# Down products of a macaron decoder layer: two of three hidden groups through seven half products, added straight from PSUM

## What is computed

```python
x = layer_norm(ALPHA * x + 0.5 * swiglu(x, ffn1_wg, ffn1_wu, ffn1_wd), ln1_g, ln1_b)
z = x @ w_in                                  # 5632 channels: C, B, h, p, g_a, g_p
m = sigmoid(g_a) * (B * conv3(C * h)) + sigmoid(g_p) * y_p     # y_p: pooling branch
x = layer_norm(ALPHA * x + m @ w_out, ln2_g, ln2_b)
x = layer_norm(ALPHA * x + 0.5 * swiglu(x, ffn2_wg, ffn2_wu, ffn2_wd), ln3_g, ln3_b)
# swiglu(x, wg, wu, wd) = (silu(x @ wg) * (x @ wu)) @ wd
```

## Time and profile before

| | |
|---|---|
| Median of three runs | 1075.14 us (1073.98 to 1077.36) |
| Profiled execution | 1076.68 us, span 1074.9 us |
| Mean granted TensorE clock | 0.992 |
| TensorE busy | 1057.1 us, 98%, 8740 matmuls |
| VectorE busy | 634.7 us, 59% |
| ScalarE busy | 436.1 us, 41% |
| GpSimd busy | 528.4 us, 49% |

### The profile page before, as it was taken

The page is one execution under the profiler, slowest core; times in us unless marked ns, Lnnn a source line. Parts: engine busy times, 40 slices in busy tenths (PEclk is TensorE's granted clock), DMA queues, the critical chain, the costliest instruction groups (busy, mean ns, idle before and its releaser), DMA issues.

```text
span 1074.9 us, 20737 instructions
## 1 busy us (share of the span) xinstructions
PE 1057.1 (98%) x8740; PEld 1051.6 (98%) x8740; DVE 634.7 (59%) x910; ACT 436.1 (41%) x659; POOL 528.4 (49%) x310
## 2 busy tenths in 40 slices
PE   7999999999999999999999999999999999999998
PEld 7999999999999999999999999999999999999997
DVE  6988711278845866722524226889884115886386
ACT  3554532155543342332332324445455123455234
POOL 4365554245657344844553546325565432565340
PEclk9999999999999999999999999989999999999999
DMA  8133244233355040532332334103335323333312
GB/s 251 37 110 102 77 118 118 79 99 111 92 142 147 2 123 2 161 99 84 97 100 84 99 111 129 41 1 99 106 93 137 88 70 99 111 91 105 99 51 80
DMA packets 195057, 103.29 MB, mean 96 GB/s; under 512 B 4420, under 2 KB 193492, under 8 KB 194957
## 3 DMA queue, kind: packets, MB, share of 16 engines
q1 hardware_dynamic: 194883, 101.85, 33.4%
q10 hardware_dynamic: 82, 0.12, 0.1%
HBM read 99.74 MB, written 2.48 MB: 95 GB/s over the span
## 4 chain that ended last, share of the span: by engine, by line
PE 89%; DVE 7%; issue 1%; ACT 1%; DMA 1%; POOL 0%; DVEq 0%; POOLq 0%; ACTq 0%
PE ps L1375 14%; PE ps L1372 14%; PE ps L1373 14%; PE ps L1355 14%; PE ps L1357 14%; PE ps L1356 14%; DVE x L1191 1%; DVE xl L956 1%; PE ps L1497 1%; DVE x L1176 1%; DMA raw<-in_ffn_wd_dram 1%; PE ps L1418 1%; PE ps L1425 1%; DVE form_lo L1007 1%; PE ps L1419 1%
## 5 line engine op out<-in xcount | busy, mean ns | idle before, releaser
L571 POOL TENSOR_TENSOR wl<-raw,wh 128x512 fp32r<-128x512 f32 x120 | 227.7, 1925 | 217.4 <-DVE raw L982 171.5
L619 ACT ACTIVATE wh<-raw 128x1024 fp32r<-128x1024 f32 (+3 forms) x203 | 238.4, 1178 | 192.7 <-DMA raw<-in_ffn_wd_dram 103.6
L1355 PE MATMUL ps<-form_hi,wh 128*128 128x260 f32 x640 | 181.5, 284 | 3.2 <-ACT temps L619 3.2
L1357 PE MATMUL ps<-form_hi,wl 128*128 128x260 f32 x640 | 181.1, 283 | 0.0
L1356 PE MATMUL ps<-form_lo,wh 128*128 128x260 f32 x640 | 180.9, 283 | 0.0
L1372 PE MATMUL ps<-xh,wh 128*128 128x260 f32 x640 | 167.0, 282 | 0.7 <-ACT yp L619 0.7
L1373 PE MATMUL ps<-xl,wh 128*128 128x260 f32 x640 | 166.5, 282 | 0.0
L563 POOL TENSOR_TENSOR wl<-raw,wh 128x1536 fp32r<-128x1536 f32 (+2 forms) x36 | 108.4, 3023 | 104.0 <-ACT wh L619 103.9
L1372 PE MATMUL ps<-hid_hi,wh 128*128 128x260 f32 x544 | 141.9, 282 | 0.0
L1373 PE MATMUL ps<-hid_lo,wh 128*128 128x260 f32 x544 | 141.8, 283 | 0.0
L1355 PE MATMUL ps<-xh,wh 128*128 128x260 f32 x480 | 136.1, 284 | 1.2 <-POOL wl L571 1.2
(11 more groups left out here) (240 smaller groups left out, 2304.1 us busy)
## 6 DMA issues: line engine op xcount, KB each, us to landing
raw<-in_ffn_wg_dram SPq DMA_DIRECT2D x80, 256.0 KB, 3.2
raw<-in_w_in_dram SPq DMA_DIRECT2D x40, 512.0 KB, 3.9
raw<-in_ffn_wd_dram SPq DMA_DIRECT2D x16, 768.0 KB, 5.3
b<-in_ffn_wu_dram SPq DMA_DIRECT2D x40, 256.0 KB, 3.4
raw<-in_ffn_wu_dram SPq DMA_DIRECT2D x40, 256.0 KB, 3.0
raw<-in_ffn_wd_dram SPq DMA_DIRECT2D x16, 640.0 KB, 5.4
raw<-in_w_out_dram SPq DMA_DIRECT2D x7, 512.0 KB, 4.0
xrow<-in_x_prompt_dram SPq DMA_DIRECT2D x4, 512.0 KB, 6.6
```

Of the source, the lines that this page charges most:

```text
L571: nc.gpsimd.tensor_tensor(wl_slot[:, s, :], raw_slot[:, s, :], wh_slot[:, s, :].bitcast(F32), ALU.subtract).then_inc(lo_ready, 1)
L619: return nc.scalar.activation(out, in_, ACT.Copy)
L1355: mm(out, hi, vh, start=start and n == 1, stop=False, skip_group_check=more)
L1357: ins = mm(out, lo, vh, start=False, stop=n == count, skip_group_check=more)
```

## The change

The 22 hidden blocks are cut in three groups of 8, 6 and 8 (`GROUPS`). The down products of the first two groups are no longer plain: two output tiles (`j`) against the group's even and odd hidden blocks form a 2 x 2 block matrix, and seven half products replace eight, exactly as for the up products. Each such "down unit" uses the machinery of an up unit: `UNITS` is the list of 28 units of an FFN, 20 up and 8 down, the four down units of a group standing behind the first up unit of the next group. `kblocks` is 4 for up units and for those of the first group, 3 for the second.

The tokens' side of the 2 x 2 matrix wants four combinations of hidden blocks. VectorE makes them from PSUM as the blocks come (`mid_sums`: one operation of 260 columns for an even block, three for an odd one), ScalarE rounds them (`round_mid`), VectorE subtracts (`mid_rest`: 3 x 260 columns, and 260 of the fourth). Of an even block only the first token half is kept as it is. The partial results of a down unit aren't copied out: VectorE adds or subtracts each of the seven straight from PSUM to or from x (`down_add`, 260 columns each), and TensorE then goes on accumulating in the same bank, after a wait for that addition. The third group (8 blocks instead of 10) stays plain, with two weight slots a tile and its lo parts in two pieces.

Other edits: T1 and T3 go to PSUM banks 6 and 7 from the third unit on; T2 is read from there, and ScalarE rounds them only after T2 is made. On VectorE the weight sums are spread out: T1/T3, T2, `rest_thirteen`, T4, then `hid_pair`, and `rest_twenty_four` moves behind `up_first`. On ScalarE the rounding of T1/T3 and of B11, B21, B22 moves ahead. At the end, the twelve extra transposes (`KEEP_WARM`) go, the square root is taken before the copy of the mean, the scale by gamma moves from VectorE to ScalarE, so that VectorE has four operations of 520 columns instead of eight of 260, and the sums of the last tile go between the transposes.

```diff
+    GROUPS = (8, 6, 8)
+    UNITS = [None]
+    for g in range(len(GROUPS)):
+        for f in range(max(GROUP_AT[g], 2), GROUP_AT[g] + GROUPS[g]):
+            UNITS.append(("up", f))
+            if g and f == GROUP_AT[g]:
+                UNITS += [("down", g - 1, j) for j in range(K // 2)]
...
+        def thirteen_whole(n, p):
+            return ps[:, 6:8, 0:kblocks(p) * P] if p > 2 else thirteen(raw_slot, n, p)
...
+            def round_thirteen(n, p):
+                act.wait_ge(t2_made if p > 2 else t13_made, unit_no(n, p))
+                if p > 2 and free[n, "T1", p]:
+                    act.wait_ge(w_used, max(free[n, "T1", p], free[n, "T3", p]))
+                copy(thirteen(wh_slot, n, p), thirteen_whole(n, p)).then_inc(t13_round, 1)
...
+                    keep(first_p, x_bank, "P1", p_taken)
+                    round_thirteen(n, p + 1)
+                    keep(first_q, z_bank, "Q5", q_taken)
+                    round_unit(n, p + 1)
+                    if was[0] == "up":
+                        second_gate(p - 1)
+                    keep(first_u, x_bank, "P6", u_taken)
+                    if was[0] == "up":
+                        hid_up(was[1], p % 2)
...
+                def mid_sums(f, pair):
+                    ...
+                    first = step.on(stt(mid32[:, 1, i, :], fourth_whole(i), -1.0, bank(pair, 1), ALU.mult, ALU.subtract))
+                    tt(mid32[:, 0, i, :], even32[:, 1, :], bank(pair, 1), ALU.subtract)
+                    dve.wait_ge(s.mid_step, first)
+                    tt(mid32[:, 2, i, :], mid32[:, 1, i, :], bank(pair, 0), ALU.add).then_inc(s.mid_made, 1)
...
+                def unit_steps(p):
+                    if was[0] == "up":
+                        up_second(p - 1)
+                    weight_sums(n, p + 1)
+                    if down:
+                        down_add("P1", p)
+                    if f in MID_NO and f % 2 == 0:
+                        mid_rests(f - 1)
+                    t_two(n, p + 1)
+                    if down:
+                        down_add("Q5", p)
+                    rest_thirteen(n, p + 1)
+                    if was[0] == "down":
+                        down_add("Q4", p - 1)
+                    last_sum(n, p + 1)
+                    if was[0] == "up":
+                        hid_pair(p - 1)
+                    if down:
+                        down_add("P6", p)
+                    mid_sums(f, pair)
+                    hid_rest(f, pair)
+                    if f is not None and f + 1 in GROUP_AT:
+                        mid_rests(f)
+                    if down:
+                        down_add("P2", p)
+                    else:
+                        gate_first(p)
+                        up_first(p)
+                    rest_twenty_four(n, p + 1)
+                    if down:
+                        down_add("Q3", p)
+                        down_add("P7", p)
...
+                    pe.wait_ge(lo_ready, lo_no[n, "B11", p])
+                    banks_free(p - 2)
+                    half_product("P1", "B11", p, x_bank)
...
+                    kept_or_added(p, "P1", 1)
+                    half_product("P6", "T2", p, x_bank, start=False)
...
-            for _ in range(KEEP_WARM):
-                nc.tensor.transpose(ps[:, 2, 0:P], ident[:], ident[:])
```

More of the change, by code:

```diff
@@ L1532, in ffn_steps @@
                 form_of = {"Q5": 0, "P6": 1, "Q3": 2, "P7": 3}
-                def half_product(name, weight, f, out, start=True):
-                    if name in form_of:
-                        vh, vl = form(form_hi, form_of[name]), form(form_lo, form_of[name])
-                    else:
-                        vh, vl = quarter(xh, *x_of[name]), quarter(xl, *x_of[name])
-                    done(run(out, [(block_of((n, weight, f), k), vh[:, k, :], vl[:, k, :]) for k in range(HK)], start=start, more=not start),
-                         n, name, f)
@@ L1632, in ffn_steps @@
-                for g, (f0, f1) in enumerate(SPANS):
-                    for f in range(f0, f1):
-                        pair(f, f0)
-                    down(g)
+                        done(run_both(DOWN_PAIR[d], tiles), n, "down", d)
+                for p in range(1, NU + 1):
+                    unit(p)
+                down_tiles()
                 def pair_free(i):
```

847 lines of the change are left out of this document (504 added, 343 removed).

## The result

The changed kernel takes 1087.16 us (median of four, 1086.56 to 1087.47) against 1075.88 us for the kernel before on the same chip: the ratio is 1.0098, 95% interval 1.0086 to 1.0109. It is 1% slower, 16 us above the prediction of 1071, and outside its range. Its profiled span is 1085.0 us, 10.1 more than before.

The account below looks back on a forecast made before the run. The prediction took TensorE's matmul stream as the bound: 1076.7 - 20.2 + 13.6 + 0.6 + 1.8 + 2.0 - 1.5 = 1073.0 us, less 1.5 for the median 1071.5, stated as 1071. The range was 1057 to 1081.

Parts of the forecast that it names:

- What bounds the kernel, and the gain: Whole kernel: TensorE's matmul stream is the limit; 168 fewer down matmuls, all on the path, save 20.2 us.
- The loop through VectorE and ScalarE: Up units, first two groups: loop of 10.4 (odd) or 10.95 us (even), mean 10.7, against TensorE's 10.09.
- The number of late units: Up units: nine an FFN late by 0.6 us, 1.4 for group ends; 6.8 an FFN, 13.6 in all.
- The short down units: Second group's down units, 63 matmuls: VectorE's additions put waits on TensorE, 0.3 us an FFN, 0.6 in all.
- the tight one: Down units: P1's addition behind the weight sums, ending in short units at 3.0 to 3.2 us, against P6 at 3.25.
- Openings and norms: FFN openings: 1.8 us more for two; norms 1 and 3: 1.4 and 0.6 us of waits for VectorE's sums.
- The end: Kernel's end: square root some 0.7 us earlier, VectorE's scaling 0.8 less with ScalarE following; -1.5 us in all.
- Rival 1: Up units: VectorE fits, ScalarE's roundings fall into existing waits, no unit late; 1058 us, chance 31%.
- Rival 2: Up units: VectorE slower still, by disturbed subtractions or costlier 1024 columns to PSUM; 9.6 us more, 1081, chance 12%.
- Rival 3: Norm 1 and late up units: TensorE's clock falls; one more fall gives 1076 us, two or more 1080 up, chance 12%.

Follow-up runs that it names:

- Experiment 2: Changed kernel with P1's addition moved ahead of the weight sums on VectorE in down units: 1088.65 us, ratio 1.0116 to the kernel before.
- experiment 6: Changed kernel with T4 formed ahead of `rest_thirteen` on VectorE in all units, down units too: 1078.48 us, ratio 1.0013 to the kernel before.
- experiment 3: Changed kernel with the weight slots of two `out` tiles exchanged in the second norm: 1083.82 us, ratio 1.0076 to the kernel before.
- experiment 7: Changed kernel with the end as before (gamma on VectorE, later square root, row block 0's transposes together, twelve extra transposes): 1088.76 us.
- experiment 9: Changed kernel with `mid_rests` behind T2, T4 ahead of `rest_thirteen` everywhere, two `out` slots exchanged, gamma on VectorE plus twelve extra transposes: 1065.82 us.
- experiments 4: Changed kernel with T4 ahead of `rest_thirteen` on VectorE in up units only: 1082.58 us, ratio 1.0066 to the kernel before.

## Why the prediction was wrong, step by step

**What bounds the kernel, and the gain.** Right: TensorE's stream, 168 matmuls fewer, none of them hidden.

**The loop through VectorE and ScalarE.** Right in mechanism and nearly in size: the mean of 10.20 and 11.30 is 10.75, predicted 10.7; units 3 to 7 and 15 to 17 have a mean distance of 10.81. `rest_thirteen` takes 1.22 to 1.23 us and its mean over 44 is the same, as predicted, but for another reason than the one given: GpSimd starts at T4, behind it, and none of the 44 runs beside GpSimd. So these say nothing on whether a PSUM operand keeps an operation clear of GpSimd; nor does the prediction's 1.70 against 0.69, which are 1024 columns and about half as many. Its 8.75 for `hid_rest` in an even block should be 8.85 by its own terms. Inside, two errors cancel: the odd loop is 0.2 shorter, the even one 0.35 longer, since GpSimd's last subtraction (the three run from 106.14 to 109.93) overlaps the first 1.05 us of the even block's `rest_twenty_four`, which takes 2.13 us instead of 1.26. By line, VectorE's groups of the kernel after (form and count, busy, mean ns, idle before):

```profile
L1124 DVE TENSOR_TENSOR wl<-raw,wh 128x1024 fp32r<-128x1024 f32 x48 | 85.5, 1782 | 3.7 <-ACT wh L703 3.7
L1096 DVE TENSOR_TENSOR ps<-raw,b 128x1024 f32<-128x1024 f32 x44 | 63.8, 1450 | 10.0 <-issue 10.0
L1119 DVE TENSOR_TENSOR wl<-ps,wh 128x1024 fp32r<-128x1024 f32 x44 | 53.9, 1225 | 47.8 <-ACT wh L703 47.8
```

**The number of late units.** This step failed, by 5.2 us in both FFNs as the table has it, 6.6 like with like. The prediction let nine units of an FFN be late and took out those that handle blocks 9, 10 and 13. Block 9, in unit 13 behind the down units, is covered, 10.10. But block 10 (unit 14) has 11.05 and block 13 (unit 17) 10.63, together 1.5 us an FFN: there is no cover left at the one and no shorter loop at the other. The first group's end (unit 8) costs 2.0 us instead of 0.6 + 0.7, and the eight units left 0.75 each instead of 0.6, 1.2 more. The second group's end falls into unit 18, in the next term.

**The short down units.** This step failed too, by the largest factor: 0.6 us predicted, or 2.0 with the second group's ends, and 8.1 measured. Neither of the two failed steps decides the sign alone (without its error the kernel would be at some 1081), both together do: they are 12.7 of the 13.8 us between -3.7 and +10.1. The other 2 us of the miss are the 1.5 taken off for the median, which after the change lies close to its profiled execution, and the rounding to 1071.

The prediction put the end of P1's addition at 3.0 to 3.2 us of a short unit, against 3.25 for P6's start, and took the small margin for enough. What it called the tight one is late in two of the four units. In unit 20 the weight sums start where it had them, 1.67 us into the unit, but take 1.30 us to the next start, beside GpSimd, instead of 0.87. With the trace's own times the loop from B22's load is 2.76 to the weight sums, 1.30, 0.41 for P1's addition, 0.15 to P6, 27 matmuls of P6, P2 and Q3 at 0.12 = 3.24, and 0.28 for the last one's end: 8.14. The distance is 8.13 (240.99 to 249.12), where 7.57 was to be had. In unit 21 the sums start 2.06 us into the unit (the 1.6 was B22's 3.06 less P7's 12 matmuls of a long unit, and a short P7 has 9), and they are 1024 columns wide, as the prediction left out. The waits of P7 and Q4 for the additions ahead of them, which it named and put at nothing, make the rest: 0.86 us in unit 22 alone. Experiment 2 showed that P1's addition is not the only one, and the gain of experiment 6 came mostly by P6's.

**Openings and norms.** TensorE waits 0.78 us for the first norm's sums (1.4 put) and for none of the third's (0.6 put). In the opening of the second FFN it waits 2.14 instead of 1.49 us, and the 0.59 for GpSimd, which should have grown, is gone. Missed is the wait in the second norm, whose code is unchanged: the slots of the `out` weights were renumbered, so that VectorE waits 3.7 us for the weights of the second FFN's unit 1 (experiment 3, 3.3 us). The prediction had gone through the waits of norms 1 and 3 and not through the order of slots.

**The end.** -1.5 us predicted; from the last closing block to the end it is 15.3 us before and 15.5 after. The step "VectorE 0.8 less, ScalarE follows" took ScalarE's operations as unchanged, and they became longer by 0.09 us each. The early square root did win its 0.7 us: from the last closing block to the finished root it is 4.68 us, in experiment 7 5.36. But the kernel before needed only 4.69, because in both of the others TensorE waits 0.45 us for ScalarE ahead of the first row transposes, which it didn't before.

**Rivals.** Rival 1 (VectorE fits) fell: it is in no up unit of the first two groups as it stood. That it can come near to fitting with a better order is what experiment 9 shows. Rival 2's named cause, disturbed subtractions in `rest_thirteen`, isn't there, though its result is. VectorE is disturbed by GpSimd elsewhere: in `rest_twenty_four` of the even blocks and in one weight sum of the short units; in the late up units the weight sums take their 1.22 us. Rival 3 can be told from the stretches: 700 to 710 us has a clock of 0.83 instead of the 0.50 of the earlier trace rows, but there are two more falls, after the wait of 2.3 us and after that of 2.14 us:

```profile
680.00:690.00 10.00, 7.70 (x59) 7.49 (x59) 7.92 (x21) 3.38 (x7) 2.41 (x2) 0.83 0.01 3
...
700.00:710.00 10.00, 8.93 (x67) 8.48 (x66) 6.60 (x17) 3.83 (x9) 2.59 (x2) 0.83 0.01 2
...
730.00:740.00 10.00, 7.86 (x53) 7.45 (x52) 9.38 (x12) 5.63 (x9) 0.00 (x0) 0.85 0.18 52
```

Lost at 1.2 GHz are three times 1.7 us (the third fall reaches into the next stretch), as much as the 5 us of the one long fall before (10.2 us at half clock; the prediction's 4.5 comes from 87 matmuls in 10 us, where 83 fit). So around the norms the clock makes no difference between the two kernels. The prediction read the mean clock of 0.992 as explained by the row at 700; that row is 5 of some 8.5 us, and the rest lies in the opening (0.88 and 0.95 in the stretches 20 to 30 and 30 to 40 us) and at the end (0.83 from 1060 to 1070), though none around 728, as it said. In the late up units of the kernel after, with one wait of 0.1 to 0.7 us in each, the clock stays at 1.00.

By a passage of the Trainium skill ("TensorE: Matmul & The Clock Gate", section "A second HAM failure mode: psum-queue depth-cycling"; the prediction names the section ahead of it) short idle times between groups of matmuls, in a kernel that cycles through PSUM banks, make the clock swing. By it the rival would hit every up stage, and that doesn't show in this trace; around the norms, with waits of 2 us, the falls are there.

## What to carry to other kernels

When work is taken off the bounding engine and handed to one that is 80% busy in the same stage, go through that engine's order and put independent work into each place where it waits: here one swap of two steps was worth some 10 us and four small edits 21 us, as much as the whole change takes from TensorE. Check every short stage on its own, from each load through the chain to the matmul that wants it, with the stage's own sizes, also those of the next stage's work that it prepares, and with disturbed durations: a margin of 0.05 us is no margin. Price every wait that the change adds, and not only the tightest. And when buffers are renumbered, look also at the stages whose code isn't touched, for a load that now starts later.

## What the runs showed of the hardware

- A VectorE operation with one PSUM and one SBUF operand is not stretched by GpSimd, as far as it was measured: 46 additions of 260 columns wholly beside GpSimd have a mean of 414 ns, 28 without it 413; in the kernel before, `hid_rest` with 520 columns has 689 ns in the 40 cases wholly beside it and 695 in four without. With 768 columns, two of experiment 9 that run beside it for 0.6 of their time take 951 and 952 ns, the undisturbed time. At 1024 columns no run here has it wholly beside GpSimd. Operations of 1024 columns with two SBUF operands reach 2.3 us beside it, 1.22 without. A result in PSUM doesn't protect an operation whose inputs are both in SBUF: the weight sums have a mean of 1450 ns (1232 before), and 0.97 or 1.39 us at 768 columns without and with GpSimd at work.
- GpSimd gains from it too: its subtraction of 512 columns took 1925 ns in the up stages before and 1438 on average over the 144 after, where VectorE has less two-operand work beside it (not tested apart).
- An activation with scale and bias both from memory takes 590 ns for 260 columns, with the bias alone 496.
- A long single wait of TensorE was nearly always followed by a fall to 1.2 GHz, a shorter one sometimes: around a wait of 1.9 to 2.8 us in the second norm in eight profiled kernels of eight, behind one of 2.1 us in the second FFN's opening in ten of eleven, behind one of 1.4 or 1.5 us there in neither of two, behind one of 0.8 us in the second norm in seven of twelve, behind one of 0.6 us there in none of five.
- The granted clock of the same stage, with the same order of work, differs between executions: 0.66 and 0.83 around 685 us in experiments 4 and 6.
